# Half of the expert table v summed through a dense coefficient matrix, the other half gathered as half rows after u's rows

## The chip, the cores and the metric

The kernel runs on one core of a Trainium2 chip. The metric is the time of one execution on the device in microseconds (us), the median of several runs. The core has TensorE (PE) with its weight loads (PEld), VectorE (DVE), ScalarE (ACT), GpSimd (POOL) and SyncE (SP), which run side by side and wait for each other by semaphores, and 16 DMA engines which SP's, ACT's and POOL's DMAs share.

## The reference

Two transformer blocks on 256 tokens of width 2048 in fp32, one after the other. The change touches only the last part of the second block, a PEER layer: every token picks 128 experts (8 heads, 16 each) out of 16384 = 128 x 128 by two lists of sub-keys, and sums rows of v with a coefficient per expert:

```python
u_sel = jnp.take(u, idx, axis=0)
a = jax.nn.gelu(jnp.einsum('thkd,td->thk', u_sel, hb), approximate=False)
v_sel = jnp.take(v, idx, axis=0)
return jnp.einsum('thk,thkd->td', (g * a).astype(hb.dtype), v_sel)
```

`idx` is 128 x (first key) + (second key), g the softmax of the 16 best scores of a head, `hb` the normalised hidden state. u and v are tables of 16384 rows of 2048 fp32 values, 8 KB a row, 134 MB each.

## The kernel before, in words

Everything up to the end of the query product is one sequence of matrix products: SP streams weights into a ring, ACT rounds them to a high part (`w_hi`), POOL or DVE makes the low part (`w_lo`), and PE multiplies high by high, high by low and low by high, since each product of rounded fp32 operands alone is not exact enough. Here only its last product, "query", matters: while it runs, DVE already picks experts.

Behind it stands the expert part. Tokens lie on the 128 partitions, in two tiles (t = 0, 1). A "row set" is one expert's row for each of the 128 tokens of a tile: POOL issues an indirect DMA with 128 indices (`gather`, L736), which brings 128 rows of 8 KB, one per partition. There are 2 x 128 row sets from u and as many from v. The work goes in four quarters hx (half of a tile's 128 experts), in each of which u's 64 row sets come first and v's 64 then, 16 buffers in eight pairs, in the fixed order of `EXPERT_PHASES`.

DVE takes each u row set's product with `hb` (`dot_products`, L1932, an operation with an accumulator that is read behind it). Then the coefficients are formed (`gates`, `coefs`, L1942 to L1952, with a gelu on ACT, L1289). v's row sets are weighed and summed in two ways: odd pairs by DVE, which adds row x coefficient to `h` (`weigh_rows`, L1962), even pairs by PE, as a product with a diagonal matrix of coefficients (L2586), which ACT builds (L1297). At the end DVE adds PE's sums to `h` (`add_sums`, L1973) and SP writes `h` out (L588).

`choose(t, c)` (L1883 to L1921) finds the experts of two heads of tile t: eight calls in all. The first two run before the first row product, the other six behind the first two rounds of v's weighings of a quarter:

```python
for hx in range(2 * TILES):
    dot_products(hx)
    coefs(hx)
    for i in range(ROUNDS):
        weigh_rows(hx, i)
        if i < 2 and hx + 1 < 2 * TILES:
            ...
            choose(t, c)
```

Each engine's program is written out by hand in its order; semaphores (`rows_full`, `rows_used`) tell when a pair of buffers is full or free.

Of the kernel before, what the change touches and what calls it, by code (L numbers as in the profile page):

```python
# [6 lines left out]
FP32 = mybir.dt.float32  # L7
# [107 lines left out]
def build(nc, A, out):  # L115
    with ExitStack() as ctx:
# [14 lines left out]
        with nc.sbuf_tensor("lasting", [P, BASE], FP32) as lasting, nc.sbuf_tensor("zone", [P, TOTAL - BASE], FP32) as zone_all:  # L131
            pass
# [204 lines left out]

        z = base
        hb = at(z, TILES, D); z += TILES * D
        gain_row = at(z, D); z += D  # L340
        pqT = at(z, 2 * E_HEADS, SEQ); z += 2 * E_HEADS * SEQ
        subk = at(z, 2 * E_HEADS, P); z += 2 * E_HEADS * P
        subkT = at(z, 2 * E_HEADS, P); z += 2 * E_HEADS * P
        xn3 = at(z, TILES, D); z += TILES * D
        scores = at(z, TILES, 2 * E_HEADS * N_KEYS); z += TILES * 2 * E_HEADS * N_KEYS
        bufs_z = z
        best1 = at(z, 2 * E_HEADS, E_TOP); z += 2 * E_HEADS * E_TOP
# [6 lines left out]

        experts = at(z, TILES, P).bitcast(U32); z += TILES * P
        dots = at(z, TILES, P); z += TILES * P
        coef = at(z, TILES, P); z += TILES * P
# [3 lines left out]
        spots = [base + n * D for n in (2, 5, 7, 8)] + [z] + [n * D for n in range(4)] + [X0 + n * D for n in range(4)]  # L361
        spots += [base + n * D for n in (3, 4, 6)]
        assert z + D <= TOTAL
        rows_buf = [at(spot, D) for spot in spots]
        junk = hot.rearrange("p a b -> p (a b)")
        diag = at(diag_at, 4, 2, P)


        PAIRS_OF_ROWS, HALF_ROWS = 8, P // 2
        ROUNDS = HALF_ROWS // (2 * PAIRS_OF_ROWS)  # L370
        EXPERT_PHASES = [(hx, table) for hx in range(2 * TILES) for table in ("peer_u_2", "peer_v_2")]
        half_slice = lambda hx: slice(hx % 2 * HALF_ROWS, (hx % 2 + 1) * HALF_ROWS)
        row_of = lambda hx, i, n, k: hx % 2 * HALF_ROWS + i * 2 * PAIRS_OF_ROWS + 2 * n + k
        dots_round, sums_round = (lambda hx, i: 2 * hx * ROUNDS + i), (lambda hx, i: (2 * hx + 1) * ROUNDS + i)
        BY_PE, BY_DVE = range(0, PAIRS_OF_ROWS, 2), range(1, PAIRS_OF_ROWS, 2)
# [28 lines left out]
        following = dict(zip(list(G)[:-1], list(G)[1:]))  # L404
        tile_full = [sem(f"tile_full{i}") for i in range(SLOTS)]
# [111 lines left out]
        def hooks(first, second, calls, ahead=0):  # L517
# [9 lines left out]
        s_qturn, s_qT2, s_ix, s_rel, s_acc2, s_sel = (sem(n) for n in (  # L527
            "queries_turned", "queryT_ready", "index_product", "relu_ready", "index_added", "selected"))
# [4 lines left out]
        s_fs, s_fp, s_fr, s_fn, s_l, s_fg, s_mg, s_erow = (sem(n) for n in (  # L533
            "fox_squares", "fox_sums", "fox_roots", "fox_normed", "stick_log", "gate2_exp", "merged_ready", "expert_rows_loaded"))
        s_sk, s_skT, s_sp, s_sc, s_bs, s_be, s_ix0, s_dot, s_gelu, s_coef, s_hb = (sem(n) for n in (
            "subkeys_turned", "subkeysT_ready", "key_scores_done", "key_scores_read", "best_shifted", "best_exp",
            "experts_ready", "dots_ready", "gelu_done", "coef_ready", "hb_ready"))
        s_diag, s_coefs = sem("diagonals_ready"), sem("coefs_ready")
        rows_full = [sem(f"rows_full{n}") for n in range(PAIRS_OF_ROWS)]
        rows_used = [sem(f"rows_used{n}") for n in range(PAIRS_OF_ROWS)]  # L540
# [4 lines left out]
        def _(sp):  # L545
# [38 lines left out]
            for t in range(TILES):  # L584
                for c in range(4):
                    cols = slice(c * CHUNK, (c + 1) * CHUNK)
                    sp.wait_ge(s_hb, TILES + 4 * t + c + 1)
                    sp.dma_start(out[0, t * P:(t + 1) * P, cols], h[:, t, cols]).then_inc(s_out, 16)  # L588
# [3 lines left out]
        def _(pool):  # L592
# [135 lines left out]
            def gather(phase, i, n, k):  # L728
# [4 lines left out]
                if k == 0 and rnd:  # L733
                    pool.wait_ge(rows_used[n], rnd)
# [1872 lines left out]
```

## Time and profile before

| | |
|---|---|
| time, median of 3 runs | 3405.6 us (3398.89 to 3405.66) |
| span of the profiled execution | 3402.5 us |
| that execution's own time beside the span | not listed apart |
| busy share PE / PEld / DVE / ACT / POOL | 74 / 58 / 52 / 32 / 69% |
| DMA | 868.10 MB, 255 GB/s in the mean |
| mean granted TensorE clock | 0.880 |

The profile page is one execution. Busy shares are means over a span with quite different stages; its 40 slices (85 us each) tell the stages apart. A line of a group names the source line, the engine, what is written and read, the number of instructions, busy time and mean duration, and the idle time before them with its releaser. In `out<-in`, "lasting" and "zone" are two large regions of SBUF, "acc" is PSUM. A timeline row begins with the start and the length in us.

### The profile page before, as it was taken

The numbers are of one execution on the slowest core, as the hardware profiler recorded it, in microseconds if no ns is written. First come the engines' busy times: TensorE is split into PE (matmuls) and PEld (weight loads), VectorE is DVE, ScalarE is ACT, GpSimd is POOL, SyncE is SP. The second block draws the span as 40 slices with busy tenths as digits, with TensorE's granted clock in tenths as the row PEclk, the third lists the DMA queues.
The fourth block names the chain that finished last, engine by engine and source line by source line (L and its number), as shares of the span: only waits on it lengthen the run. The fifth ranks groups of instructions, "written<-read, shape, count | busy, mean of one in ns | idle before, by whom it ended". The sixth has DMA issues, their size and how long they took to land.

```text
span 3402.5 us, 42238 instructions
## 1 busy us (share of the span) xinstructions
PE 2507.2 (74%) x15833; PEld 1974.7 (58%) x15833; DVE 1781.8 (52%) x2456; ACT 1081.7 (32%) x2108; POOL 2364.1 (69%) x1677
## 2 busy tenths in 40 slices
PE   7999996989999999989999899108503730571077
PEld 5777885779988998889988679103201310230032
DVE  4375656242200223220412446997797879778954
ACT  6444424464444444454546554000000100000000
POOL 7400316859999999987866579886687578568853
PEclk9999997999999999999999999559856965796589
DMA  5684300546655665555544346999999999999998
GB/s 180 206 237 145 105 3 26 185 123 183 185 191 187 183 183 185 187 153 161 161 131 125 117 164 206 396 427 427 427 428 427 427 427 427 428 426 427 427 427 344
DMA packets 241376, 868.10 MB, mean 255 GB/s; under 512 B 18940, under 2 KB 21484, under 8 KB 174886
## 3 DMA queue, kind: packets, MB, share of 16 engines
q0 software_dynamic: 73776, 536.97, 37.5%
q1 hardware_dynamic: 163414, 316.11, 30.6%
q10 hardware_dynamic: 4016, 12.75, 1.3%
q8 instruction: 106, 1.74, 0.2%
q14 instruction: 64, 0.52, 0.0%
HBM read 860.24 MB, written 2.10 MB: 253 GB/s over the span
## 4 chain that ended last, share of the span: by engine, by line
PE 50%; POOL 19%; DMA 11%; DVE 7%; issue 4%; ACT 1%; DVEq 0%; ACTq 0%; POOLq 0%; SPq 0%
PE acc L2022 20%; PE acc L2032 19%; DMA zone<-in_peer_v,zone 10%; POOL lasting L736 10%; POOL zone L736 9%; PE acc L2028 3%; PE acc L2160 3%; PE acc L2586 2%; POOL w_lo L616 1%; DVE lasting L1962 1%; DMA lasting<-in_peer_u,zone 1%; PE acc L2475 1%; DVE zone L1568 0%; PE acc L2069 0%; DVE x_lo L1697 0%
## 5 line engine op out<-in xcount | busy, mean ns | idle before, releaser
L616 POOL TENSOR_TENSOR w_lo<-lasting,w_hi 128x512 fp32r<-128x512 f32 x1024 | 1372.4, 1359 | 276.0 <-ACT w_hi L785 257.3
L785 ACT ACTIVATE w_hi<-lasting 128x512 fp32r<-128x512 f32 (+1 forms) x1184 | 741.3, 631 | 903.6 <-PE acc L2022 457.0
L2586 PE MATMUL acc<-zone,lasting 128*128 128x512 f32 x512 | 256.3, 655 | 694.3 <-ACT lasting L1297 643.4
L2586 PEld LDWEIGHTS acc<-zone,lasting 128*128 128x128 f32 x512 | 105.2, 210 | 841.6 <-ACT lasting L1297 505.2
L2032 PE MATMUL acc<-x_hi,w_hi 128*128 128x256 f32 (+1 forms) x1856 | 305.5, 286 | 11.5 <-DVE x_lo L1697 4.3
L736 POOL DMA_INDIRECT zone<-in_peer_v,zone x128 | 192.2, 1502 | 165.6 <-DVE lasting L1962 73.6
L1932 DVE CUSTOM_DVE_ANT_0 zone<-zone 128x2048 f32<-128x2048 f32 x128 | 293.4, 2292 | 21.9 <-DMA zone<-in_peer_u,zone 7.1
L1932 DVE CUSTOM_DVE_ANT_0 zone<-lasting,zone 128x2048 f32<-128x2048 f32 x128 | 293.5, 2293 | 21.0 <-DMA lasting<-in_peer_u,zone 8.6
L2032 PE MATMUL acc<-x_lo,w_hi 128*128 128x256 f32 (+1 forms) x1856 | 298.6, 283 | 0.0
L2032 PE MATMUL acc<-x_hi,w_lo 128*128 128x256 f32 (+1 forms) x1856 | 298.3, 283 | 0.0
L2586 PE MATMUL acc<-lasting 128*128 128x512 f32 x512 | 247.8, 635 | 64.9 <-DMA zone<-in_peer_v,zone 38.2
L736 POOL DMA_INDIRECT lasting<-in_peer_u,zone x128 | 248.5, 1942 | 58.4 <-issue 36.9
L736 POOL DMA_INDIRECT zone<-in_peer_u,zone x128 | 256.7, 2005 | 42.7 <-issue 37.8
L2032 PEld LDWEIGHTS acc<-x_hi,w_hi 128*128 128x128 f32 x1856 | 255.0, 189 | 19.1 <-issue 7.7
L2032 PEld LDWEIGHTS acc<-x_lo,w_hi 128*128 128x128 f32 x1856 | 255.3, 189 | 0.0
L2032 PEld LDWEIGHTS acc<-x_hi,w_lo 128*128 128x128 f32 x1856 | 254.4, 189 | 0.0
L736 POOL DMA_INDIRECT lasting<-in_peer_v,zone x128 | 199.5, 1558 | 72.7 <-issue 35.6
L1289 ACT ACTIVATE zone<-zone 128x64 f32<-128x64 f32 x4 | 1.0, 256 | 744.7 <-DVEq L1936 744.7
L2022 PE MATMUL acc<-w_hi,x_hi 128*128 128x512 f32 (+1 forms) x672 | 216.0, 403 | 19.5 <-DVE w_lo L1379 8.8
L2586 PEld LDWEIGHTS acc<-lasting 128*128 128x128 f32 x512 | 101.3, 203 | 209.4 <-issue 196.3
L2022 PE MATMUL acc<-w_hi,x_lo 128*128 128x512 f32 (+1 forms) x672 | 211.1, 396 | 0.0
L2022 PE MATMUL acc<-w_lo,x_hi 128*128 128x512 f32 (+1 forms) x672 | 209.6, 393 | 0.0
(419 smaller groups left out, 3951.7 us busy)
## 6 DMA issues: line engine op xcount, KB each, us to landing
lasting<-in_w_in SPq DMA_DIRECT2D x200, 512.0 KB, 3.7
lasting<-in_w_up SPq DMA_DIRECT2D x128, 512.0 KB, 3.8
lasting<-in_w_down SPq DMA_DIRECT2D x128, 512.0 KB, 3.6
lasting<-in_w_mix_out SPq DMA_DIRECT2D x32, 512.0 KB, 3.6
lasting<-in_w_out SPq DMA_DIRECT2D x32, 512.0 KB, 3.6
lasting<-in_peer_w_query SPq DMA_DIRECT2D x32, 512.0 KB, 3.7
lasting<-in_w_kv_cross SPq DMA_DIRECT2D x16, 512.0 KB, 3.7
lasting<-in_w_q_cross SPq DMA_DIRECT2D x8, 512.0 KB, 3.7
```

Source lines behind the costliest of these rows:

```text
L616: pool.tensor_tensor(w_lo[:, k, 0:width], ring[:, slot, s % SLOT_SLABS, 0:width], w_hi[:, k, 0:width].bitcast(FP32), ALU.subtract).then_in ...
L736: pool.indirect_dma_start(out=rows_buf[2 * n + k], out_offset=None, in_=A[table][0], in_offset=bass.IndirectOffsetOnAxis(ap=experts[:, hx ...
L785: act.activation(w_hi[:, s % PARTS, 0:width], ring[:, slot, s % SLOT_SLABS, 0:width], ACT.Copy).then_inc(hi_ready, 1)
L1289: act.activation(part, part, ACT.Gelu).then_inc(s_gelu, 1)
L1932: last = dve.tensor_tensor_reduce(out=junk, in0=rows_buf[2 * n + k], in1=hb[:, t], scale=1.0, scalar=0.0, op0=ALU.mult, op1=ALU.add, accum ...
L1962: last = STT(h[:, t], rows_buf[2 * n + k], coef[:, t, slot:slot + 1], h[:, t], ALU.mult, ALU.add)
L2022: last = pe.matmul(bank(banks[t])[:, 0:width], xp[:, s, g.lo + t * P:g.lo + (t + 1) * P], wp[:, k, 0:width], **kw)
L2028: last = pe.matmul(bank(banks[f // 2])[:, f % 2 * SEQ:(f % 2 + 1) * SEQ], wp[:, k, f * P:(f + 1) * P], xp[:, s, g.lo:g.hi], skip_group_che ...
L2032: last = pe.matmul(bank(banks[f])[:, 0:g.hi - g.lo], wp[:, k, f * P:(f + 1) * P], xp[:, s, g.lo:g.hi], **kw)
L2160: return pe.matmul(out, lhsT, rhs, start=start, stop=stop, skip_group_check=check)
L2475: last = pe.matmul(two_out(m), probT2[0:size, m % 2, n * P:(n + 1) * P], v, start=n == 0, stop=n == t + 1)
L2586: last = pe.matmul(bank(4 * t + c), diag[:, n // 2, k], rows_buf[2 * n + k][:, c * CHUNK:(c + 1) * CHUNK], start=hx % 2 == 0 and i == 0 an ...
```

## The change

It concerns only what follows the query product. v's columns are split in half.

- All 256 row sets of u are gathered first, one after the other, with nothing of v between (`gather_u`, `dot_product`). There are 14 buffers for tile 0's and 8 for tile 1's. The six later choices of experts stand behind the row products 40, 64, 88, 104, 118 and 126, the coefficients behind 66, 129, 220 and 255. A choice has two more small operations, for the numbers of half rows.
- The left half of v (columns 0 to 1023) isn't gathered. For each token a 128 x 128 matrix of coefficients is built, second key by first key: two one-hot matrices over the token's 128 experts, one scaled by the coefficient, are multiplied by PE, four tokens to a group, and ACT copies the result to SBUF (`dense`, 128 KB a partition). For tile 0 ACT makes the one-hots, while u's rows are still coming; for tile 1 DVE does, behind the last row product.
- In 128 steps SP then streams v's left half once, 128 rows of 4 KB a step. ACT makes the high parts of the tile (1024 columns) and of the 256 coefficients `dense[:, :, i]`, DVE the low parts of 768 columns and of the coefficients, POOL that of the other 256 columns, and PE does 12 matmuls (3 products, 2 tiles of tokens, 2 x 512 columns).
- The right half of v (columns 1024 to 2047) is gathered in the same 128 steps as half rows of 4 KB (`gather_v`), two row sets a step, four buffers. DVE weighs them all (`weigh_half_row`, 128 x 1024). PE no longer weighs rows, and ACT makes no diagonals.

The core of the diff:

```diff
+        FIRST_TILE, SECOND_TILE = (5, 7, 8, 13, 4, 6, 0, 1, 9, 10, 11, 12, 14, 15), (5, 7, 8, 13, 4, 16, 17, 18)
+        half_rows = [at(half_rows_at + n * HALF_D, HALF_D) for n in range(4)]
+        CHOOSE_AFTER = {40: (0, 2), 64: (0, 3), 88: (1, 0), 104: (1, 1), 118: (1, 2), 126: (1, 3)}
+        COEFS_AFTER = {66: 0, 129: 1, 220: 2, 255: 3}
+        BY_DVE = 768
...
+            for i in range(N_KEYS):
+                if i == 0:
+                    sp.wait_ge(s_dot, 2 * TILES)
+                if i == 2:
+                    sp.wait_ge(s_dense, GROUPS)
+                if i >= 4:
+                    sp.wait_ge(s_vlo_dve, i - 3)
+                    sp.wait_ge(lo_ready, V_SLAB + i - 3)
+                sp.dma_start(v_raw[:, i % 4], A["peer_v_2"][0][i * P:(i + 1) * P, 0:HALF_D]).then_inc(tile_full[i % 4], 16)
...
+            def gather_v(q):
+                t, j, b = q // P, q % P, q % 4
+                if q >= 4:
+                    pool.wait_ge(s_wdve, q - 4 + 1)
+                else:
+                    pool.wait_ge(s_dotted, 4)
+                pool.indirect_dma_start(
+                    out=half_rows[b], out_offset=None, in_=v_halves,
+                    in_offset=bass.IndirectOffsetOnAxis(ap=half_rows_no[:, t, j:j + 1], axis=0)
+                ).then_inc(v_full[b], 16)
...
+            for i in range(N_KEYS):
+                if i == 0:
+                    pool.wait_ge(s_dot, 2 * TILES)
+                while done < min(U_SLOTS, 4 + (i * (U_SLOTS - 4)) // (N_KEYS - 4)):
+                    gather_v(done)
+                    done += 1
+                pool.wait_ge(hi_ready, V_SLAB + i + 1)
+                pool.tensor_tensor(v_lo[:, i % 2, BY_DVE:], v_raw[:, i % 4, BY_DVE:], v_hi[:, i % 2, BY_DVE:].bitcast(FP32),
+                                   ALU.subtract).then_inc(lo_ready, 1)
...
+            for i in range(N_KEYS):
+                act.wait_ge(tile_full[i % 4], 16 * (TURNS + i // 4 + 1))
+                if i >= 2:
+                    act.wait_ge(slab_used, PARTS + V_SLAB + i - 1)
+                act.activation(v_hi[:, i % 2], v_raw[:, i % 4], ACT.Copy)
+                act.activation(dense_now[:, 0, i % 2], dense[:, :, i], ACT.Copy).then_inc(hi_ready, 1)
...
+            def one_hots(g):
+                dve.wait_ge(s_dense, g - 1)
+                for n in range(4):
+                    s_ = 4 * (g - GROUPS // TILES) + n
+                    TS(hot_of(g, 0)[:, n], key_no, keysT[:, 2, s_:s_ + 1], None, ALU.is_equal)
+                    last = TS(hot_of(g, 1)[:, n], key_no, keysT[:, 3, s_:s_ + 1], coefT[:, 1, s_:s_ + 1], ALU.is_equal, ALU.mult)
+                last.then_inc(s_hot, 1)
...
+            for i in range(N_KEYS):
+                dve.wait_ge(hi_ready, V_SLAB + i + 1)
+                TT(v_lo[:, i % 2, 0:BY_DVE], v_raw[:, i % 4, 0:BY_DVE], v_hi[:, i % 2, 0:BY_DVE].bitcast(FP32), ALU.subtract)
+                TT(dense_now[:, 1, i % 2], dense[:, :, i], dense_now[:, 0, i % 2].bitcast(FP32), ALU.subtract).then_inc(s_vlo_dve, 1)
+                while done < ((i + 1) * U_SLOTS) // N_KEYS:
+                    weigh_half_row(done)
+                    done += 1
...
+                    for n, (cp, vp) in enumerate(((0, v_hi), (1, v_hi), (0, v_lo))):
+                        for t in range(TILES):
+                            for c in range(2):
+                                last = pe.matmul(bank(2 * t + c), dense_now[:, cp, k, t * P:(t + 1) * P], vp[:, k, c * CHUNK:(c + 1) * CHUNK],
+                                                 start=first and k == 0 and n == 0, stop=final and k == 1 and n == 2)
```

How this moves instructions is shown at three places. On DVE, behind the first quarter's coefficients (L1952), before:

```order
L1952 TENSOR_TENSOR zone<-zone 128x64
L1962 SCALAR_TENSOR_TENSOR lasting<-zone,lasting 128x2048 x2
L1962 SCALAR_TENSOR_TENSOR lasting<-lasting,zone 128x2048 x4
L1962 SCALAR_TENSOR_TENSOR lasting<-zone,lasting 128x2048 x2
L1883 MAX zone<-zone 128x8
```

The choice (from L1883) stands between weighings of v. In the changed kernel it stands between row products of u; this is DVE's order around product 40, whose L2054 is the row product, 128x1 its accumulator, and L1999 the start of the choice:

```order
L2054 ISA zone<-zone 128x2048
L2054 ISA zone 128x1
L1999 MAX zone<-zone 128x8
L2000 MAX_INDEX zone<-zone 128x8
L2002 MATCH_REPLACE zone<-zone 128x128
```

The weighings have moved behind all products. On DVE where tile 1's one-hots (L2079, L2080) end and the 128 steps begin, in the changed kernel:

```order
L2079 TENSOR_SCALAR lasting<-lasting 128x128
L2080 TENSOR_SCALAR lasting<-lasting 128x128
L2118 TENSOR_TENSOR w_lo<-lasting,w_hi 128x768
L2119 TENSOR_TENSOR x_hi<-dense,x_hi 128x256
L2087 SCALAR_TENSOR_TENSOR lasting<-zone,lasting 128x1024 x2
L2118 TENSOR_TENSOR w_lo<-lasting,w_hi 128x768
```

Each step is four DVE operations on one queue. On POOL's queue, from the last gathers of u (L791) on, in the changed kernel (L805 is the gather of a half row set, L828 POOL's low part):

```order
L791 DMA zone<-in_peer_u,lasting 128x2048 x5
L805 DMA zone<-in_peer_v,lasting 128x1024 x4
L828 TENSOR_TENSOR w_lo<-lasting,w_hi 128x256
L805 DMA zone<-in_peer_v,lasting 128x1024 x2
L828 TENSOR_TENSOR w_lo<-lasting,w_hi 128x256
```

Two gathers and one low part alternate on POOL, where gathers alone stood before.

## Rows read from the trace of the kernel before

**Rows 1.** The page: 40 slices of 85 us, busy tenths, GB/s.

```profile
PE   7999996989999999989999899108503730571077
...
DMA  5684300546655665555544346999999999999998
GB/s 180 206 237 145 105 3 26 185 123 183 185 191 187 183 183 185 187 153 161 161 131 125 117 164 206 396 427 427 427 428 427 427 427 427 428 426 427 427 427 344
```

**Rows 2.** Busy PE, PEld, DVE, ACT, POOL; granted clock, DMA share, GB/s.

```profile
2134.00:3397.00 1263.00, 501.38 (x1045) 208.64 (x1043) 998.19 (x1028) 57.29 (x149) 890.01 (x506) 0.71 1.00 422
```

**Rows 3.** The page: the DMA queue of POOL's gathers: packets, MB, share.

```profile
q0 software_dynamic: 73776, 536.97, 37.5%
```

**Rows 4.** The page: the chain that ended last, by line.

```profile
PE acc L2022 20%; PE acc L2032 19%; DMA zone<-in_peer_v,zone 10%; POOL lasting L736 10%; POOL zone L736 9%; PE acc L2028 3%; PE acc L2160 3%; PE acc L2586 2%; POOL w_lo L616 1%; DVE lasting L1962 1%; DMA lasting<-in_peer_u,zone 1%; PE acc L2475 1%; DVE zone L1568 0%; PE acc L2069 0%; DVE x_lo L1697 0%
```

**Rows 5.** DVE's timeline: the first row products (start, length).

```profile
2134.32 2.29 DVE L1932 CUSTOM_DVE_ANT_0 zone<-zone 128x2048 f32<-128x2048 f32 x1
2136.53 0.08 DVE L1932 DVE_READ_ACCUMULATOR2_ANT zone<- 128x1 f32 x1
2136.73 2.29 DVE L1932 CUSTOM_DVE_ANT_0 zone<-zone 128x2048 f32<-128x2048 f32 x1
```

**Rows 6.** DVE's timeline: a choice's first operation, and what follows it.

```profile
2326.30 0.30 DVE L1883 MAX8 zone<-zone 128x8 f32<-128x128 f32 x1
...
2344.72 4.78 DVE L1962 SCALAR_TENSOR_TENSOR lasting<-zone,lasting 128x2048 f32<-128x2048 f32 x2
```

**Rows 7.** ACT's groups by form (busy us, mean ns), then its timeline.

```profile
L1001 ACT ACTIVATE zone<-acc 128x512 f32<-128x512 f32 x16 | 9.6, 598 | 11.1 <-PE acc L2160 10.0 <-PE acc L2193 1.1
L1289 ACT ACT_TABLE_LOAD x4 | 5.1, 1283 | 0.1
L1218 ACT ACTIVATE zone<-zone 128x1024 f32<-128x1024 f32 x4 | 4.2, 1044 | 0.0
...
2290.80 2.45 ACT L1297 ACTIVATE lasting<-lasting,zone 128x128 f32<-128x128 f32 x8 [0.84 <-DVEq L1953]
```

**Rows 8.** DVE's groups by form over the whole span.

```profile
L1379 DVE TENSOR_TENSOR w_lo<-lasting,w_hi 128x512 fp32r<-128x512 f32 x144 | 96.4, 690 | 81.7 <-ACT w_hi L785 80.6
L1379 DVE TENSOR_TENSOR w_lo<-lasting,w_hi 128x368 fp32r<-128x368 f32 x16 | 8.2, 538 | 4.7 <-ACT w_hi L785 4.6
L1584 DVE TENSOR_SCALAR zone<-zone 128x128 f32<-128x128 f32 x1 | 0.2, 228 | 0.0
```

**Rows 9.** POOL's timeline: a gather beside DVE's products, one alone.

```profile
2137.73 2.11 POOL L736 DMA_INDIRECT lasting<-in_peer_u,zone  x1 [0.30 <-issue]
...
3301.17 0.94 POOL L736 DMA_INDIRECT lasting<-in_peer_v,zone  x1 [0.30 <-issue]
```

**Rows 10.** POOL's groups by form: a product of 256 columns.

```profile
L659 POOL TENSOR_TENSOR zone<-zone 128x256 f32<-128x256 f32 x6 | 4.4, 735 | 0.5
```

**Rows 11.** DVE's, then POOL's timeline at 2121 us.

```profile
2121.19 4.97 DVE L1918 TENSOR_TENSOR zone<-zone 128x512 f32<-128x512 f32 x1
...
2121.84 3.77 POOL L616 TENSOR_TENSOR w_lo<-lasting,w_hi 128x512 fp32r<-128x512 f32 x3
```

**Rows 12.** PE's timelines: at granted clock 1.00, after two idle times.

```profile
1101.15 0.63 PE L2022 MATMUL acc<-w_hi,hid_lo 128*128 128x512 f32 x2
1101.61 0.64 PE L2022 MATMUL acc<-w_lo,hid_hi 128*128 128x512 f32 x2
...
3299.00 7.11 PE L2586 MATMUL acc<-lasting 128*128 128x512 f32 x16 [1.31 <-DMA lasting<-in_peer_v,zone]
...
3308.74 5.37 PE L2586 MATMUL acc<-lasting 128*128 128x512 f32 x8 [2.63 <-DMA zone<-in_peer_v,zone]
```

**Rows 13.** DVE's timeline: the last additions of the sums.

```profile
3397.05 2.48 DVE L1973 TENSOR_TENSOR lasting<-acc,lasting 128x512 f32<-128x512 f32 x4 [0.26 <-issue]
```

**Rows 14.** A DMA issue (KB, us to landing); a stretch as rows 2.

```profile
lasting<-in_w_down SPq DMA_DIRECT2D x128, 512.0 KB, 3.6
...
900.00:1000.00 100.00, 100.00 (x587) 87.91 (x586) 14.54 (x16) 44.93 (x71) 96.63 (x74) 1.00 0.60 189
```

More of the change, by code:

```diff
@@ L378, in build @@
+        dense = dense_all.rearrange("p (t i) -> p t i", i=N_KEYS)
+        GROUPS = TILES * P // 4
+        one_hot = at(D, 2, 2 * 4 * P)
+        hot_of = lambda g, k: one_hot[:, g % 2, k * 4 * P:(k + 1) * 4 * P].rearrange("p (n c) -> p n c", n=4)
+        v_raw = at(0, 4, HALF_D)
+        v_hi, v_lo = (part_at(RING + n * PARTS * CHUNK, 2, HALF_D) for n in range(2))
+        dense_now = parts[X0][:, 0:1024].rearrange("p (k s t) -> p k s t", k=2, s=2)
+        BY_DVE = 768
         G = {}
@@ L404, in build @@
         following = dict(zip(list(G)[:-1], list(G)[1:]))
+        TURNS = sum(g.turns * g.bodies for g in G.values())
         tile_full = [sem(f"tile_full{i}") for i in range(SLOTS)]
@@ L741, in _, with gather_u @@
-            early = [(0, 0), (0, 1), (1, 0), (1, 1), (2, 0)]
-            rests("query", after={at_: lambda n=n, k=k: gather(0, 0, n, k) for at_, (n, k) in zip(((2, 15), (3, 2), (3, 5), (3, 8), (3, 11)), early)})
+            def gather_u(q):
+                t, j, b = q // P, q % P, U_BUF[q]
+                if j % 32 == 0:
+                    pool.wait_ge(s_ix0, q // 32 + 1)
+                if U_USE[q]:
+                    pool.wait_ge(s_dotted, U_BEFORE[q] + 1)
+                if b in (16, 17):
+                    pool.wait_ge(s_ix0, 4 * TILES)
+                elif b == 18:
+                    pool.wait_ge(s_dot, 2)
+                pool.indirect_dma_start(
+                    out=u_rows[b], out_offset=None, in_=A["peer_u_2"][0],
+                    in_offset=bass.IndirectOffsetOnAxis(ap=experts[:, t, j:j + 1], axis=0)
+                ).then_inc(u_full[U_SEM[q]], 16)
@@ new lines, in _ @@
+            exp_gates(2)
+            exp_gates(3)
+            gelu_dots(1)
+            act.wait_ge(s_keysT, 1)
+            act.activation(keysT.rearrange("p k s -> p (k s)"), bank(6), ACT.Copy).then_inc(s_keysR, 1)
+            act.wait_ge(s_coefs, 2)
+            act.wait_ge(s_keysR, 1)
+            read_coefs(0)
+            for g in range(GROUPS // TILES):
+                one_hots(g)
+                if g:
+                    read_dense(g - 1)
+            read_dense(GROUPS // TILES - 1)
@@ L1880, in _ @@
                 step(dve.memset(iota16[:, k:k + 1], float(k)))
+            step(dve.memset(work1[:, 0:P], 1.0))
+            step(dve.tensor_tensor_scan(key_no, work1[:, 0:P], work1[:, 0:P], -1.0, ALU.add, ALU.bypass))
             def best16(val, idx, src):
@@ new lines, in dense_group @@
+            def dense_group(g):
+                pe.wait_ge(s_hot, g + 1)
+                if g >= 2:
+                    pe.wait_ge(s_denseR, g - 1)
+                for n in range(4):
+                    last = pe.matmul(bank(6 + g % 2)[:, n * P:(n + 1) * P], hot_of(g, 1)[:, n], hot_of(g, 0)[:, n], start=True, stop=True)
+                last.then_inc(s_dense, 1)
+            pe.wait_ge(s_keys, 1)
+            for k in range(2 * TILES):
+                last = pe.transpose(bank(6)[:, k * P:(k + 1) * P], split_keys[:, k], ident)
@@ L2593 @@
+            v_tiles(0, first=True)
+            loop(pe, N_KEYS // 2 - 1, v_tiles, 1)
+            v_tiles(N_KEYS // 2 - 1, final=True)
 def kernel(**inputs):
```

285 lines of the change are left out of this document (163 added, 122 removed).

## The prediction

> **What bounds the kernel now.** I first read the page's 40 slices [rows 1]. Through the matrix products TensorE is at nine tenths and the DMA engines at about six; from slice 26 (2130 us) to the end the DMA engines stand full at 427 GB/s and TensorE is mostly idle. Next the stretch 2134 to 3397 [rows 2]: DMA share 1.00, DVE busy 998 of 1263 us, POOL 890, PE 501. By queue [rows 3], q0, which holds POOL's gathers, carries 536.97 MB: 256 row sets from u and 256 from v, each 128 rows of 8 KB, 1.05 MB, so 2.456 us at 427 GB/s. 512 of them are 1257 us. The chain of waits alternates there between landing v rows and POOL's gathers [rows 4]. So the last 1263 us are bound by bytes, with DVE second at 79%. Whether fewer bytes help depends on what DVE must do besides.
>
> When its row is there, a DVE row product starts every 2.42 us [rows 5]: practically the gather's 2.456 us.
>
> **Part 1, the u stage.** Bytes: 268 MB, as before, 629 us. DVE now does all 256 row products in one go: 256 x 2.42 = 620 us. Six of the eight choices of experts lie among them. One choice lasts from 2326.30 to 2344.72 = 18.42 us [rows 6]; six are 110.5, and the two small operations added to each (0.2 us each) make 113. Before, the choices ran inside the time in which DVE waited for v's rows; that cover is gone, since v's rows are no longer gathered beside u's. Buffers (14, then 8) let the DMA run ahead during a choice, but DVE is never faster afterwards than 2.42 us a row, so it doesn't catch up. Three sets of coefficients (about 1.1 each) and the splitting of the keys (1) add 4. DVE's sum is 737 us against 629 of DMA: **DVE becomes the bound**, and the DMA idles some 108 us. The first product starts at 2134.3 now [rows 5], and the two small operations added to the choice ahead of it put it off by 0.4. End: 2134.7 + 737 = 2872.
>
> Tile 0's one-hots on ScalarE hide: 12 operations of 0.31 us, one 128x1024 of 1.04 and one PSUM read of 0.60 are 5.4 us a group, 172 us for 32 groups [rows 7], between product 129 and product 220, whose 91 products take 220. If that cover were gone, up to 172 us would be bare.
>
> **Part 2, tile 1's dense coefficients.** Behind the last product: the gelu (an ACT table load of 1.28 [rows 7] and a short operation), the last coefficients and two transposes, 4 us. Then DVE builds 32 groups of one-hots, 8 operations of 128x128 each. The one such row is 0.228 us [rows 8]; the next operation may start 0.08 us before the end of the last [rows 5]. Bounds: 8 x (0.228 - 0.08) = 1.2 us a group, and with 0.06 for each start 2.3. I take the middle, 1.75, 56 us; the ends are 38 and 74. PE (four small matmuls) and ACT (0.60) have less to do per group. The DMA holds only four half row sets and two v tiles here: nothing hides it. With 3 us until the first tile is split: 2872 + 4 + 56 + 3 = 2935.
>
> **Part 3, the v stage**, 128 steps. Each brings one dense tile (0.52 MB) and two half row sets (0.52 MB each): 1.573 MB, 3.68 us at 427 GB/s. That is 201 MB where 268 were gathered, so 67 MB or 157 us less; this is the gain that is offered. Per step the engines have:
> - DVE: the low part of 768 columns. 512 columns take 0.690 us and 368 take 0.538 [rows 8], 1.056 ns a column, so 0.96, with 0.04 to the next operation 1.00. The low part of the coefficients, 256 elements each 512 bytes from the next: no row has such a stride; from below contiguous 256, by the same two rows 0.42, plus 0.04; from above 512 contiguous, 0.73. Unlike any row, so I take the middle, 0.60. Two weighings of 1024 columns: two of 2048 take 4.78 [rows 6], less 1024 x 1.056 each, 1.31 apiece, 2.62. Sum 4.22.
> - POOL: two gathers of 0.95 us bare and 0.30 between [rows 9], and the low part of 256 columns, 0.735 [rows 10]. Both hold off or wait for DVE: at 2121.19 a DVE product of 0.69 us took 4.97, until three POOL products that ended at 2125.61 were through [rows 11], and gathers last 2.11 beside DVE products, 0.94 alone [rows 9]. The gathers don't lengthen DVE's products (the 2.42 holds beside them), so I charge DVE only POOL's product, 0.78.
> - DVE with that: **5.0 us a step**. Below, 4.08 if the stride is free and POOL's product fits in a gap.
> - PE: 12 matmuls of 512 columns. At granted clock 1.00 two start every 0.46 us [rows 12], so 2.8 us; at the lower of the two levels, 5.6.
> - ACT: 128x1024, 1.04, and 128x256, below the 0.60 of 512 [rows 7]; 1.6 at most.
> 128 x 5.0 = 640 us: 2935 + 640 = 3575. From the first addition of the sums to the end is 5.4 us now [rows 13]; with the last matmuls 7. End 3582, 179.5 us behind 3402.5. The page has no time for its execution beside this span; the median of the three runs is 3.1 above it. So 3405.6 + 179.5 = **3585 us**.
>
> The stride is where a page speaks against the change. The Trainium skill, "Vector Engine (DVE) Microarchitecture Reference", measured stream behaviour, gives 1.73 ns a column, not 1.054, when one source hops every element. By it the 256-wide operation takes about 0.6 us, as in my sum; by the contiguous rows it is 0.46 and the total 18 us less.
>
> **The rivals.**
> A. The bytes stay the bound, **faster**. 2134.7 + 629 + 60 + 471 + 7 = 3302, reported 3305. For it: share 1.00 in [rows 2]. Against it: DVE's own operations after 2134, at the cheapest, are 737 + 4 + 38 + 128 x 4.08 = 1301 us, more than the 1263 that the whole stretch takes. It would need a step of under (3402 - 7 - 2935)/128 = 3.6 us, where its own operations need 4.08. 3%.
> B. Cheaper steps, 4.1 to 4.8 us: 3470 to 3560. POOL's product may slip in where DVE waits anyway, and the stride may be free. 23%.
> C. Dearer steps, 5.4 to 6.5 us: 3636 to 3777. There are only four half row buffers: a set is gathered when the one four earlier is weighed, so two steps must hold a weighing, POOL's gather (up to 2.4 us behind DVE's operations) and the landing. A 512 KB load of SP's lands in 3.6 us [rows 14]; above 7 us, with two others in flight, the loop passes 5.4 a step. The same range comes from PE at its lower clock: after 2.63 us of idling 8 matmuls took 5.37 us, after 1.31 us 16 took 7.11 [rows 12]; my steps leave PE 2.2 us idle, between the two. PE then needs at most 5.6. 24%.
> D. Packets of 4 KB. 2 KB packets moved 189 GB/s at share 0.60 [rows 14], 315 GB/s when full; at that a step needs 5.0 us of DMA, total 3585 again, inside my range but with the DMA full and not DVE. Half way to the 8 KB packets' 427 it is 4.2 and not the bound. Of the forecast's 50% I count 8 for it. The Trainium skill, "DMA: Bandwidth & Descriptors", measured bandwidth, asks for DMAs of 1 MiB for three quarters of the peak. These are half that; by it a step would need at least 4.9 us and the total would be no less than about 3570. No run here shows half row gathers yet; the 189 GB/s of 512 KB loads in [rows 14] were asked for by the products and are no ceiling.
> That the bytes aren't saved is no rival: 128 tiles of 0.52 MB and 256 half sets are fixed by the code.
>
> **How the numbers follow.** Forecast, steps of 4.8 to 5.4: 50%, own range 3560 to 3636. B 23, C 24, A 3. The range 3490 to 3720 leaves out A, the lowest fifth of B and the highest third of C, some 15 to 20%. About 0.2% (7 us) is what can be told from no change. Faster 3%, within it 1% (a step of just 3.6), slower 96%.
>
> **What would show it.** In the changed profile: DVE busy at 9 tenths or more from 2134 to the end but for a short stage near 2875 to 2935, where the GB/s fall to nearly nothing; in the u stage GB/s of about 365 in the mean (268 MB in 737 us), not 427; row products 2.42 us apart; in the v stage about 315 GB/s, a period of 5.0 us, the low part of 768 columns lengthened now and then by POOL's. If the GB/s stand at 427 in both stages, A is right. If DVE idles before its weighings for a DMA, it is C's buffers or D (D with share 1.00); if ACT waits for PE and the granted clock is near 0.5, C's clock. A u stage of under 700 us would mean that the choices are hidden after all, and then my first term is wrong.

## The result and the profile after

The changed kernel takes 3912.3 us (3909.4 to 3922.4 in four runs) against 3402.2 for the kernel before (3397.2 to 3405.7, four runs on the same chip): a ratio of 1.150, 95% interval 1.148 to 1.152. The forecast was slower, at 3585 us with a range up to 3720. The sign was right, the size was not: 327 us more than forecast.

The page's 40 slices of the changed kernel (98 us each), to be held against [rows 1]:

```profile
## 2 busy tenths in 40 slices
PE   7999979999999999999987000033036666544434
...
DVE  4376562422012222222447999999999866553333
ACT  5444235544444545545653000079013322221111
POOL 7200348699999998776578766378828755542222
PEclk9999989999999999999999555555578877776666
DMA  5764005466566555554357988489938877663333
GB/s 178 236 196 150 4 12 172 142 184 190 189 181 186 185 190 152 156 147 124 116 168 265 393 357 341 184 350 427 427 150 307 306 252 244 232 211 129 123 120 127
```

In the first 30 slices, up to 2931 us, it reads as forecast: DVE at nine tenths from 2130 on, then the short stage near 2900 with little DMA. In the last ten the GB/s do not stand still. They start at 307, fall to about 240 and end near 125, and every engine's digit falls with them. No engine is full at the end.

Windows of the changed kernel (columns: stretch, its length, busy us and count of PE, PEld, DVE, ACT, POOL; then granted clock, DMA share, GB/s), as in [rows 2]:

```profile
2135.00:2800.00 665.00, 68.01 (x261) 57.92 (x261) 625.08 (x847) 169.86 (x458) 461.44 (x224) 0.50 0.85 352
2950.00:3050.00 100.00, 69.65 (x252) 50.12 (x252) 92.13 (x85) 32.03 (x41) 85.23 (x63) 0.93 0.91 324
3200.00:3300.00 100.00, 63.22 (x192) 46.98 (x190) 64.73 (x63) 25.58 (x32) 56.55 (x47) 0.77 0.74 251
3400.00:3500.00 100.00, 53.19 (x175) 40.23 (x174) 56.80 (x56) 22.44 (x28) 54.51 (x44) 0.74 0.69 232
3700.00:3800.00 100.00, 41.16 (x98) 29.38 (x97) 31.45 (x32) 12.62 (x16) 29.01 (x24) 0.64 0.38 126
```

The first row is the u stage: DVE busy for 625 of 665 us. The others are the v stage. DVE's four operations a step show how many steps fit into 100 us. The same view with DVE's low parts of v alone (L2118, one a step) counts them:

```profile
2960.00:3080.00 120.00, 23.96 (x25) 0.96 0.93 331
3085.00:3285.00 200.00, 30.47 (x32) 0.77 0.76 256
3285.00:3491.00 206.00, 28.74 (x30) 0.75 0.67 229
3510.00:3880.00 370.00, 28.75 (x30) 0.64 0.39 129
```

That is 4.8, 6.3, 6.9 and 12.3 us a step, for steps that all do the same work: three plateaus, the second (6.5 in the mean) with a small step up inside it. Single operations didn't lengthen: 23.96/25 and 28.75/30 are both 0.96 us. So the extra time is waiting. The waits from 2960 to 3900:

```profile
engine line waited for: us in total, times, longest us
ACT w_hi L1413 <- PE acc L2748: 742.3, 121, 12.3
...
PE acc L2748 <- POOL w_lo L828: 445.0, 87, 8.7
POOL zone L805 <- DVE lasting L2087: 433.9, 84, 9.1
DVE w_lo L2118 <- ACT x_hi L1414: 416.7, 66, 9.8
```

It is a ring: ACT waits for PE, PE for POOL's low part, POOL's gather for DVE's weighing, DVE for ACT. DVE waits for the DMA 1.1 us in all: the half rows are there. One step of the last plateau, from the timeline (start, length, engine; in brackets the idle time before it):

```profile
3601.30 1.06 ACT L1413 ACTIVATE w_hi<-lasting 128x1024 fp32r<-128x1024 f32 x1 [10.37 <-PE acc L2748]
...
3602.91 0.96 DVE L2118 TENSOR_TENSOR w_lo<-lasting,w_hi 128x768 fp32r<-128x768 f32 x1 [7.93 <-ACT x_hi L1414]
...
3604.29 2.65 DVE L2087 SCALAR_TENSOR_TENSOR lasting<-zone,lasting 128x1024 f32<-128x1024 f32 x2
3605.83 1.93 POOL L805 DMA_INDIRECT zone<-in_peer_v,lasting  x1 [8.15 <-DVE lasting L2087]
3607.78 0.73 POOL L828 TENSOR_TENSOR w_lo<-lasting,w_hi 128x256 fp32r<-128x256 f32 x1
3608.57 3.78 PE L2748 MATMUL acc<-w_hi,x_hi 128*128 128x512 f32 x8 [7.36 <-POOL w_lo L828]
...
3612.15 1.79 PE L2748 MATMUL acc<-w_lo,x_hi 128*128 128x512 f32 x4
3614.03 1.06 ACT L1413 ACTIVATE w_hi<-lasting 128x1024 fp32r<-128x1024 f32 x1 [11.15 <-PE acc L2748]
```

ACT, DVE, DVE's first weighing, POOL's gather, POOL's low part, PE, ACT: each starts when the one before it is through, 12.7 us from one w_hi to the next, and PE's 12 matmuls take 5.6 us (granted clock 0.53 over them, which is near the lower of its two levels).

**The theory** then was this. POOL's program puts its gathers ahead of its low part of step i by a schedule that the diff shows, `min(256, 4 + (i * 252) // 124)`: 4 + 2.032 a step, while DVE weighs 2 a step. Gather n needs the buffer that weighing n - 4 frees. At first the gathers ahead of POOL's low part of step i need weighings of steps before i. From i = 31 the schedule is one ahead of 2 a step: gather 2i + 4 stands ahead of the low part of step i and needs weighing 2i, of step i itself. From i = 62 it is two ahead and needs weighing 2i + 1. From i = 93 it needs weighing 2i + 2, of step i + 1: PE's step i can't begin until DVE is in step i + 1, for which ACT must have rounded tile i + 1. The double buffers of high and low parts are then worth nothing. The places fit. A low part of POOL's that is late in step i delays DVE in step i + 2, since ACT's tile i + 2 waits for PE's tile i; so DVE's intervals should lengthen behind its steps 32, 63 and 94. They do behind 32, 64 and 94. The first plateau would end at 2933 + 32 x 4.8 = 3087 (in the trace step 32 starts at 3085), the second at 3087 + 62 x 6.5 = 3490 (step 94 starts at 3491), the third at 3490 + 34 x 12.3 = 3908, the span's end; the small step up inside the second lies at step 64, 3285.

The sizes fit as well. One trip round the ring takes the 12.7 us of the step above. Three steps share a trip while POOL's low part of step i needs a weighing of step i - 1, two from i = 31 on, one from i = 93 on. As an estimate from the 12.7 that is 4.2, 6.4 and 12.7 us a step. Measured are 12.3 in the last plateau and 6.3 to 6.9 in the second, where DVE's steps come in pairs, a short one of 4.1 us and a long one of 7.8 to 9.9. In the first plateau DVE's own work is longer than 4.2 and hides the ring.

Three rivals: PE's lower clock makes the steps long and the rest follows; small transfers land too late in four buffers (C of the prediction); 4 KB packets (D).

### The profile page after: what moved, and what is told of

The parts are those of the page before. It is cut to its first block, busy times and chain, and to the rows that moved or that the text cites. A ratio compares the mean times of both kernels' runs of the same rounds, so it can differ in the third digit from the quotient of the medians.

```text
span 3907.7 us, 46617 instructions
## 1 busy us (share of the span) xinstructions
PE 2623.1 (67%) x16863; PEld 2229.4 (57%) x16863; DVE 2074.9 (53%) x3116; ACT 1422.7 (36%) x2715; POOL 2472.8 (63%) x1805
## 4 chain that ended last, share of the span: by engine, by line
PE 49%; DVE 28%; POOL 7%; ACT 4%; issue 3%; DVEq 1%; DMA 1%; ACTq 0%; SPq 0%
PE acc L2157 17%; PE acc L2167 16%; DVE zone L2054 15%; PE acc L2748 8%; POOL zone L805 5%; PE acc L2163 2%; DVE lasting L2087 2%; PE acc L2295 2%; POOL w_lo L828 2%; ACT w_hi L1413 2%; DVE w_lo L2118 2%; ACT x_hi L1414 1%; DVEq L2088 1%; DVE lasting L2080 1%; PE acc L2610 1%
## 5 line engine op out<-in xcount | busy, mean ns | idle before, releaser
L805 POOL DMA_INDIRECT zone<-in_peer_v,lasting x256 | 373.3, 1458 | 490.8 <-DVE lasting L2087 437.1
L2748 PE MATMUL acc<-w_hi,x_hi 128*128 128x512 f32 x1024 | 376.5, 528 | 455.9 <-POOL w_lo L828 449.0
L2748 PEld LDWEIGHTS acc<-w_hi,x_hi 128*128 128x128 f32 x1024 | 257.7, 262 | 562.3 <-POOL w_lo L828 495.7
L1413 ACT ACTIVATE w_hi<-lasting 128x1024 fp32r<-128x1024 f32 x128 | 135.4, 1058 | 759.6 <-PE acc L2748 759.5
L791 POOL DMA_INDIRECT zone<-in_peer_u,lasting x136 | 277.2, 2039 | 145.2 <-DVE lasting L2039 56.0
L2087 DVE SCALAR_TENSOR_TENSOR lasting<-zone,lasting 128x1024 f32<-128x1024 f32 x256 | 345.9, 1351 | 13.1 <-DMA zone<-in_peer_v,lasting 1.2
L2118 DVE TENSOR_TENSOR w_lo<-lasting,w_hi 128x768 fp32r<-128x768 f32 x128 | 122.7, 958 | 426.9 <-ACT x_hi L1414 421.4
L2054 DVE CUSTOM_DVE_ANT_0 zone<-zone 128x2048 f32<-128x2048 f32 x136 | 311.8, 2293 | 18.2 <-issue 0.7
L791 POOL DMA_INDIRECT lasting<-in_peer_u,lasting x120 | 244.5, 2037 | 68.4 <-issue 35.4
L2054 DVE CUSTOM_DVE_ANT_0 zone<-lasting,zone 128x2048 f32<-128x2048 f32 x120 | 275.1, 2293 | 16.1 <-issue 0.8
```

Of the source, the lines that this page charges most:

```text
L791: pool.indirect_dma_start(out=u_rows[b], out_offset=None, in_=A["peer_u_2"][0], in_offset=bass.IndirectOffsetOnAxis(ap=experts[:, t, j:j + ...
L805: pool.indirect_dma_start(out=half_rows[b], out_offset=None, in_=v_halves, in_offset=bass.IndirectOffsetOnAxis(ap=half_rows_no[:, t, j:j + ...
L1413: act.activation(v_hi[:, i % 2], v_raw[:, i % 4], ACT.Copy)
L2054: dve.tensor_tensor_reduce(out=junk, in0=u_rows[b], in1=hb[:, t], scale=1.0, scalar=0.0, op0=ALU.mult, op1=ALU.add, accum_out=dots[:, t, j ...
L2087: STT(h[:, t, HALF_D:], half_rows[b], coef[:, t, j:j + 1], h[:, t, HALF_D:], ALU.mult, ALU.add).then_inc(s_wdve, 1)
L2118: TT(v_lo[:, i % 2, 0:BY_DVE], v_raw[:, i % 4, 0:BY_DVE], v_hi[:, i % 2, 0:BY_DVE].bitcast(FP32), ALU.subtract)
```

## The experiments

**Two gathers a step.**

```diff
-                while done < min(U_SLOTS, 4 + (i * (U_SLOTS - 4)) // (N_KEYS - 4)):
+                while done < min(U_SLOTS, 4 + 2 * i):
```

> POOL's list of gathers goes by 4 + 2 per step instead of 4 + 2.032 per step; nothing else changes. Theory 1 (drift: with four half row buffers the gathers that stand ahead of POOL's low part of step i wait in the end for weighings of step i itself, then of step i+1, and everything turns serial): the first plateau, 4.8 us a step, holds to the end. v stage 2933 + 128 x 4.85 + 9, about 3563 us in all, 3540 to 3600. Theory 2 (TensorE's lower clock makes it the bound and the rest follows): the steps lengthen all the same, about 3900. Theory 3 (landing of small transfers in four buffers): no change either, about 3900.

Measured: 3567.7 us, ratio to the kernel before 1.049 (1.047 to 1.051). One window early and one late in its v stage:

```profile
2950.00:3050.00 100.00, 73.06 (x241) 53.02 (x240) 89.48 (x83) 32.11 (x40) 81.95 (x62) 0.85 0.91 320
3400.00:3500.00 100.00, 69.78 (x248) 50.50 (x249) 90.37 (x83) 33.20 (x42) 82.97 (x62) 0.91 0.92 323
```

The plateau holds to the end, 4.83 us a step in the mean of 127, and 345 us are gone by one expression. Rivals that promised about 3900 fall, in so far as they are to explain the 345.

**Three gathers ahead from the second step on.**

```diff
-                while done < min(U_SLOTS, 4 + (i * (U_SLOTS - 4)) // (N_KEYS - 4)):
+                while done < min(U_SLOTS, 7 + 2 * i if i else 4):
```

> POOL's list of gathers is put three ahead of 2 per step from the second step on, the lead that the drift reaches only from about step 94. Theory 1 (drift): 12.6 to 12.7 us a step from the start of the v stage, 2933 + 128 x 12.6 + 9, about 4550 us. Theories 2 and 3 (TensorE's clock, landing of transfers): one more gather issued early changes nothing, about 3900, with steps that still lengthen along the way.

Measured: 4513.9 us (one run), 12.3 us a step. A window from its start and one from its end:

```profile
2950.00:3050.00 100.00, 41.17 (x96) 29.25 (x96) 31.45 (x32) 12.62 (x16) 28.84 (x25) 0.64 0.39 129
4300.00:4400.00 100.00, 41.85 (x96) 29.58 (x96) 30.77 (x33) 12.62 (x16) 28.27 (x25) 0.64 0.38 126
```

The last plateau can be had from the start, with the same bytes, packets and buffers: eight steps in 100 us, granted clock 0.64. So the clock fell because the steps had turned serial: the first experiment's kernel has the same PE work at 0.85 and 0.91. What the lower clock cost on top is inside the 12.7 us (5.6 us of PE for the 2.8 that full clock needs); it is not a cause of its own.

**Half of each row product.** DVE multiplies only columns 0 to 1023 of u's rows.

```diff
-                dve.tensor_tensor_reduce(out=junk, in0=u_rows[b], in1=hb[:, t], ...
+                dve.tensor_tensor_reduce(out=junk[:, 0:HALF_D], in0=u_rows[b][:, 0:HALF_D], in1=hb[:, t, 0:HALF_D], ...
```

> Leaves out half of each row product with u (columns 1024 to 2047), so the dot products and the gates are those of half the columns; gathers and all else as in the changed kernel. Theory (u stage bound by DVE, choices bare): a product takes about 1.2 us, DVE has 256 x 1.3 + 113 = 446 us to do, and the gathers set the pace: last product at about 2135 + 630 = 2765 us instead of 2867, total about 100 us shorter than the changed kernel, about 3810. Rival (u stage held by POOL's or the gathers' own pace below 427 GB/s): last product later than 2820.

Measured: 3817.7 us (one run), the last product at 2776 instead of 2867. In this kernel's u stage DVE has time to spare and the DMA is nearly full (same columns as above):

```profile
2135.00:2760.00 625.00, 67.98 (x261) 57.88 (x261) 411.52 (x889) 171.54 (x461) 251.05 (x245) 0.50 0.97 409
```

This is Part 1 turned round: with DVE's work below the DMA's, the choices are hidden and the stage is bound by bytes. In the changed kernel some 91 us of them are bare (2867 less 2776).

**GpSimd without its product.** As the first, with all 1024 columns of the low part on DVE.

```diff
-        BY_DVE = 768
+        BY_DVE = 1024
...
-                pool.wait_ge(hi_ready, V_SLAB + i + 1)
-                pool.tensor_tensor(v_lo[:, i % 2, BY_DVE:], ...
```

> As the run with 2 gathers per step, and besides DVE computes the low part of all 1024 columns of each v tile, POOL only gathers. Priced by the sum of DVE's own operations: low part 1.35, coefficients 0.62, weighings 2.62, together 4.6 a step: about 2933 + 128 x 4.6 + 9 = 3531 us. If POOL's product holds DVE by the 0.78 that I charged, this is 0.4 to 0.5 us a step faster than the run with 2 gathers per step (50 to 60 us). Rival (POOL's product slips in where DVE waits): equal or slower, by up to the 0.27 of the added columns, 35 us.

Measured: 3589.6 us, ratio 1.054 (1.052 to 1.056), 22 us more than with POOL's product. The theory's 3531 fell. The weighings did get shorter, as it said, from 1.48 us in the mean to 1.28 (the first experiment's kernel, then this one, both 2960 to 3550):

```profile
2960.00:3550.00 590.00, 361.20 (x244) 0.93 0.92 324
...
2960.00:3550.00 590.00, 299.69 (x234) 0.88 0.89 312
```

A step in which DVE waits for nothing takes 4.4 us from one low part to the next. But the mean step is 5.0 us; the time went into two waits, of the same stretch:

```profile
POOL zone L804 <- DVE lasting L2083: 241.0, 189, 2.7
...
DVE lasting L2083 <- DMA zone<-in_peer_v,lasting: 81.3, 75, 2.4
```

POOL, no longer held by a product, comes to each gather before its buffer is free, and DVE now waits for half rows to land, where the first experiment's kernel had 13.9 us of that. The gathers' count and median time from issue to landing, in the first experiment's kernel and then in this one:

```profile
zone<-in_peer_v,lasting POOLq DMA_INDIRECT x243, 6.4
...
zone<-in_peer_v,lasting POOLq DMA_INDIRECT x235, 7.4
```

This reads as C's loop through four buffers: with 1.5 us from a weighing's start to the gather that it lets go and 7.4 to the landing, some 9 of the 10 us of two steps are taken, so DVE's saving could not be had. Why the landing takes 1 us longer here stays open, and that it is the loop alone was not tried with more buffers.

**Unsplit products.** As the first, and PE multiplies the coefficients and v in plain fp32. No high or low parts are left.

```diff
-                    for n, (cp, vp) in enumerate(((0, v_hi), (1, v_hi), (0, v_lo))):
...
+                            last = pe.matmul(bank(2 * t + c), dense_now[:, k, t * P:(t + 1) * P], v_raw[:, k, c * CHUNK:(c + 1) * CHUNK],
```

> As the run with 2 gathers per step, but TensorE multiplies the coefficients and v unsplit in fp32: the low parts of v and of the coefficients fall away on VectorE and GpSimd, ScalarE only copies the coefficient slice; VectorE keeps the two weighings, 2.65 a step. TensorE needs 8 passes of 0.444 us, read from the fp32 products of the kernel before (16 in 7.11 us), if each 512-column product of fp32 counts two such records: 4 x 2 x 0.444 = 3.55 a step. Theory (v stage was bound by VectorE with GpSimd's product; the bytes are next): DMA 3.68 a step at 427 GB/s, about 2933 + 128 x 3.7 + 9 = 3416 us, 3405 to 3440, GB/s near 427 in the v stage. Rival (half row gathers of 4 KB packets can't reach 427 GB/s: 315 to 325 was a ceiling of the DMA): no faster than 4.8 a step, about 3560, with the DMA share at 1.00. Rival (TensorE falls to its lower clock): up to 7.1 a step, 3850.

Measured: 3487.9 us, ratio 1.026 (1.024 to 1.027): 80 us less than the first, 72 more than the theory's. Two windows show why both:

```profile
3300.00:3350.00 50.00, 50.00 (x118) 22.20 (x117) 29.91 (x24) 9.09 (x14) 23.46 (x24) 1.00 1.01 398
...
3390.00:3470.00 80.00, 0.00 (x0) 0.00 (x0) 53.95 (x43) 0.00 (x0) 52.10 (x43) 0.50 0.83 276
```

The DMA had not been the bound at 4.8 us a step: with the low parts gone, the bytes flow at 398 GB/s. (The edit takes work off DVE, POOL and ACT at once and frees PE from waiting for them, so it doesn't tell DVE's part from theirs.) But v's tiles, which nothing ties to the half rows any more, ran ahead: PE was through with its 128 tiles before 3385, and the last 50 or so half row sets came alone, at 276 GB/s, one each 1.9 us. That is again the loop through four buffers, now bare for about 90 us. PE was busy for the whole of the first window, 3.43 us a step (eight records of 0.43), against 3.55 expected.

**Half rows into the u stage.** The other half of the forecast's loss is the DMA's idle time beside the choices. As the run before, but the first 80 half row sets are weighed by PE, as the kernel before did it, and gathered where DVE chooses experts.

```diff
+        EARLY = {102: 16, 118: 32, 132: 64}
+        BY_PE = 80
...
+                while done < EARLY.get(q, 0):
+                    gather_v(done)
+                    done += 1
```

> As the run with unsplit fp32 products, and the first 80 half row sets of the first tile are weighed by TensorE (a diagonal of coefficients times the half rows, two 512-column fp32 products each, 1.78 us by the kernel before): 64 of them are gathered in the u stage, 16, 16 and 32 behind the row gathers 102, 118 and 132, where VectorE is away for its choices and the DMA queue idles; 16 between the dense groups of the second tile. VectorE weighs the other 176. Theory (the u stage is VectorE's, its choices leave the DMA some 108 us of idle time that half rows can fill): u stage as long as before within 10 us, v stage bound by TensorE's fp32 products at 3.43 a step as seen in the run before this one, 2935 + 439 + 9 = 3383 us, 3375 to 3400, faster than the kernel before the change by about 0.6%. Rival (GpSimd's gathers, 64 more in the u stage, or TensorE at its lower clock hold up the row gathers): the u stage grows by 30 us or more, about 3415 and slower than the kernel before.

Measured: 3443.0 us, ratio 1.012 (1.009 to 1.014). The v stage came out as written (PE busy throughout), the u stage as the rival had it: the last product began at 2924. Its waits from 2400 to 2900:

```profile
POOL zone L808 <- PE acc L2740: 71.6, 33, 19.1
DVE zone L2062 <- DMA zone<-in_peer_u,lasting: 49.0, 7, 47.6
```

A block of 32 stands in POOL's queue ahead of the second tile's row gathers, POOL waits in it for PE, and DVE then waits 47.6 us in one piece. It is the fault of the changed kernel once more: a gather that waits holds up what is queued behind it.

**The same, spread.** One half row set behind each of 44 row gathers, 16 in one block, 16 among the dense groups.

```diff
-        EARLY = {102: 16, 118: 32, 132: 64}
-        BY_PE = 80
+        EARLY = {q: q - 87 if q < 132 else 60 for q in range(88, 133)}
+        BY_PE = 76
```

> As the run with 80 early half row sets, with 76 of them by TensorE and otherwise placed: one behind each of the row gathers 88 to 131, 16 behind gather 132 and 16 among the second tile's dense groups, so that no block of 32 stands ahead of the row gathers of the second tile. In the run before VectorE waited 47.6 us in one piece and 14 more behind such blocks, and the u stage ended at 2927 instead of 2869. Theory (the blocks did it): u stage ends at 2870 to 2880, dense groups 65 us, v stage 440 to 445 bound by TensorE's fp32 products, in all about 3390 us, 3380 to 3405. Rival (the extra gathers themselves are too much for GpSimd or TensorE in the u stage): no better than 3430.

Measured: 3403.1 us, ratio 1.000 (0.999 to 1.001): level with the kernel before. 40 us came from moving these gathers (and four fewer of them). The v stage ends in PE alone, with DVE and POOL through:

```profile
3350.00:3390.00 40.00, 40.00 (x95) 17.70 (x94) 0.00 (x0) 7.08 (x11) 0.00 (x0) 1.00 0.49 158
```

**Every fourth tile in split halves**, to relieve PE.

```diff
+                    products = [(dense_now[:, k % 2], v_raw[:, k])] if k < 3 else [
+                        (dense_parts[:, 0], v_hi), (dense_parts[:, 1], v_hi), (dense_parts[:, 0], v_lo)]
```

> As the run with the spread half row sets, and every fourth v tile is multiplied in three products of split halves as in the changed kernel (TensorE 2.8 us instead of 3.43), VectorE making both low parts, 1.27 + 0.60 for such a tile. TensorE's v stage 96 x 3.43 + 32 x 2.8 = 419 us instead of 440; the bytes, 180 half sets and 128 tiles, 161 MB, are 420 us at the 385 GB/s that such a mix moved at share 1.00. Theory: about 20 us less than the run before, 3370, 3355 to 3395, and faster than the kernel before the change by 0.5 to 1%. Rival (the bytes at 4 KB packets are the bound already): same as the run before within 8 us.

Measured: 3418.7 us, ratio 1.005 (1.003 to 1.006), 16 us worse than the spread run. Neither theory had this. Over most of its v stage the DMA moved 353 GB/s, where the spread run had 390 in the same stretch, and PE was no longer busy all the time:

```profile
2960.00:3350.00 390.00, 367.06 (x992) 186.54 (x991) 246.12 (x213) 98.41 (x139) 203.05 (x154) 1.00 0.95 353
```

PE now waited 25.2 us for DVE's low part of a coefficient slice, which stands in DVE's queue behind weighings that wait for rows. The part that each wait has in the 16 us stays open.

**Fewer early sets.**

```diff
-        EARLY = {q: q - 87 if q < 132 else 60 for q in range(88, 133)}
-        BY_PE = 76
+        EARLY = {**{q: q - 87 for q in range(88, 124)}, 132: 52}
+        BY_PE = 52
```

> As the run with the spread half row sets, but TensorE weighs 52 instead of 76: one behind each of the row gathers 88 to 123, 16 behind gather 132, none among the second tile's dense groups. In the spread run VectorE and the gathers were through 53 us before TensorE's last product, room for 24 more sets at 2.08 us each, 50 us; the u stage ended 16 us later than in the changed kernel (2885 for 2869), and the dense groups took 65 us instead of 58. Theory (both were the price of the early sets): u stage ends at about 2875, dense groups 58 us, v stage 440 us by TensorE, in all 10 to 17 us less than the spread run, 3386 to 3393, and 0.3 to 0.5% faster than the kernel before the change. Rival (the gathers become the end of the v stage): 3400 or more, the same as before.

Measured: 3393.2 us (3384.9 to 3401.4, 12 runs), ratio 0.998 (0.997 to 0.999): the first version that is faster than the kernel before, by 0.2%, at the edge of what can be told. Against the spread run it gained 0.2%, each held against the kernel before on its own chip: some 7 us, where the theory had 10 to 17. Its profiled execution was its fastest run. There the u stage ended at 2875, as the theory had it, and the first fp32 product of the v stage came at 2938, so the dense groups still took 63 us and not 58; two windows:

```profile
2875.00:2938.00 63.00, 39.28 (x258) 32.97 (x259) 61.34 (x263) 20.30 (x36) 1.31 (x1) 0.94 0.07 20
...
3300.00:3350.00 50.00, 50.00 (x118) 22.12 (x117) 29.07 (x23) 9.43 (x15) 24.26 (x23) 1.00 1.00 392
```

PE and the DMA are both full in the v stage; the run with every fourth tile in split halves relieved PE alone and gained nothing. The largest loss left is the second tile's dense groups, 63 us in which the DMA moves 20 GB/s.

## Why the prediction was right and wrong

**What bounds the kernel**, that the gain was bytes and DVE was second: right. The half product run shows that the u stage is bound by bytes once DVE has less to do than the DMA, and the unsplit run the same of the v stage, where PE is full too.

**Part 1, the u stage ends at 2872**: right. The last rows of the changed kernel's stage, in the pattern of [rows 5]:

```profile
2864.36 2.29 DVE L2054 CUSTOM_DVE_ANT_0 zone<-zone 128x2048 f32<-128x2048 f32 x1 [0.48 <-issue]
...
2866.79 2.29 DVE L2054 CUSTOM_DVE_ANT_0 zone<-zone 128x2048 f32<-128x2048 f32 x1
```

Products 2.43 us apart, the stage over at 2869, 352 GB/s up to 2800 where about 365 had been written. DVE waited for no DMA and no other engine in it. Part of the good fit is luck: the first product came at 2128.0, 6.7 us earlier than written, and the stage took 741 us instead of 737. The half product run confirms the cause.

**Part 2, tile 1's coefficients, 56 us (38 to 74)**: right, 58 us from 2871.2 to 2929.3. The first low part of the v stage began at 2933.1 for 2935.

**Part 3, 5.0 us a step throughout**: this is the step that failed, and in it POOL's line: "POOL: two gathers of 0.95 us bare and 0.30 between". I wrote the schedule down as two a step and asked only what POOL's operations cost, not what they wait for and what is queued behind that wait. The schedule is 2.032 a step. Rival C even has the condition, that a set is gathered when the one four earlier is weighed, but prices only the landing with it. Set against two weighings a step, 252 gathers in 124 steps with four buffers would have shown the low parts of v behind a gather that waits for the same step's weighing, and at last for the next step's. The drift cost 3912.3 - 3567.7 = 345 us, more than the whole miss; without it the forecast is 17 us (0.5%) too high.

That remainder is in the period, 4.8 for 5.0, and its smallness is partly luck. DVE's own terms held. From the first plateau's timeline, a step without waiting, 4.43 us from one L2118 to the next:

```profile
2981.18 0.96 DVE L2118 TENSOR_TENSOR w_lo<-lasting,w_hi 128x768 fp32r<-128x768 f32 x1
...
2982.05 0.60 DVE L2119 TENSOR_TENSOR x_hi<-dense,x_hi 128x256 fp32r<-128x256 f32 x1
...
2982.58 2.94 DVE L2087 SCALAR_TENSOR_TENSOR lasting<-zone,lasting 128x1024 f32<-128x1024 f32 x2
...
2983.45 0.99 POOL L828 TENSOR_TENSOR w_lo<-lasting,w_hi 128x256 fp32r<-128x256 f32 x1
```

The low part of 768 columns takes 0.87 to the next start (forecast 1.00), the strided 256 columns take 0.60 (0.60) and 0.53 to the next start, the two weighings 2.94 with POOL's product inside them and 2.65 without (2.62 had been written). In this step POOL's product holds DVE by 0.3 us. In others, where the product falls into the first weighing, it is up to 1.0; in the mean of the first experiment's kernel it is 2 x (1.48 - 1.28) = 0.4 us a step, by the rows shown for the run without POOL's product, and not the 0.78 that I charged from [rows 11], where three of its products followed each other. In place of the other 0.4 came waits that the sum put at nothing, DVE's in the first experiment's kernel, 2960 to 3550, 122 steps:

```profile
DVE w_lo L2118 <- ACT x_hi L1414: 21.2, 21, 1.8
DVE lasting L2087 <- DMA zone<-in_peer_v,lasting: 13.9, 26, 1.8
```

These are 0.3 us a step. So the period came out near the forecast because an overpriced term and a missing one nearly cancel. The Trainium skill, "Vector Engine (DVE) Microarchitecture Reference", measured stream behaviour, gives its 1.73 ns a column for hops of 4 KiB, and the step here is 512 bytes. Put in place of the contiguous rate it gives an estimate of 0.6 us for 256 columns; 0.60 was measured, so the trace agrees for this step too.

**The rivals.** A is out: DVE's sum ruled it out as written. B (steps of 4.1 to 4.8) touches what the kernel does without the drift, whose 3567.7 us lie in the forecast's own range of 3560 to 3636. C named the four buffers and the lower clock, and its signs came (DVE idle, ACT waiting for PE, clock down), yet it is not what happened: its loop was the landing of transfers, and in the changed kernel DVE waited 1.2 us for half rows in the whole v stage. Its price, up to 6.5 us a step, knew nothing of a step in which each engine waits for the next. Its 5.4 us a step for a landing above 7 us was too dear as well: without POOL's product the median landing was 7.4 us and the step 5.0. The landing loop shows only once the drift is gone and DVE is relieved, in the run without POOL's product and at the end of the unsplit one. D is out too: the same 4 KB packets moved 398 GB/s in the unsplit run. The Trainium skill, "DMA: Bandwidth & Descriptors", measured bandwidth, asks for 1 MiB a DMA to reach three quarters of the peak. Here DMAs of half of that, several in flight, moved 398 GB/s, 93% of the 427 that gathers of whole rows reach [rows 1], and the measurement decides.

**What would show it** was written as two states, a period of 5.0 or DVE idle for a DMA. A fall in plateaus was not among them, and it is what told the cause here: the effect grew with the loop's index, and the schedule that counts at another rate was what grew with it.

## What to carry to other kernels

Where one in-order queue holds both gathers that wait for a buffer and work that others wait for, compare the two rates over the whole loop, to the last step: a lead that grows by one in 31 steps ends in a step where everything is serial. Write for each gather which step's work frees its buffer, and keep it behind the work of that step. Then count how many steps share one trip round the ring of waits: the period is the trip divided by that count. Fewer bytes pay only as far as the second engine's sum allows; here four changes had to come together (schedule, unsplit products, early sets, their spreading) before 67 MB less gave 0.2%.

## What the runs showed of the hardware that was not expected

Plain fp32 products of 512 columns cost 0.86 us at full clock (3.43 us for four), against 0.69 for the three split ones (0.23 each [rows 12]); PE pays a quarter more and DVE, ACT and POOL are spared their low and high parts. Tiles and half rows together, both in packets of 4 KB, reached 389 GB/s over 2950 to 3380 of the unsplit run and 394 over 2940 to 3360 of the last one, at a DMA share of 1.00 and 1.01, where whole rows of 8 KB had 427: 8 to 9% less with the engines full. That it is the size of the packets alone wasn't tried. Half row sets alone through four buffers moved 276 GB/s at a share of 0.83. And taking work off POOL made the kernel slower by 22 us, though POOL's product had been what PE waited for most. One product of 256 columns on POOL lengthened DVE's two weighings by 0.4 us in the mean.
